# Down-projection bias of a MoE layer moved from the expert stage to the last stage, with two output buffers by chunk

## What is computed

```python
gu = xb @ w_gu[e] + b_gu[e]
gate = jnp.minimum(gu[:, :D_EXPERT], SWIGLU_LIMIT)
up = jnp.clip(gu[:, D_EXPERT:], -SWIGLU_LIMIT, SWIGLU_LIMIT)
act = (up + 1.0) * (gate * jax.nn.sigmoid(SWIGLU_ALPHA * gate))
y = act @ w_down[e] + b_down[e]
out[token] += gates[token, e] * y
```

## Time and profile before

| what | value |
|---|---|
| median of three executions | 2579.87 us |
| the profiled execution | 2585.97 us |
| its span from first to last instruction | 2584.3 us |
| busy PE, DVE, ACT, POOL | 2225.3, 1617.1, 1283.1, 578.6 us |
| stage 5 (868 to 942 us) | 74 us |
| stage 6 (942 to about 2500 us) | 1558 us |
| stage 7 (2513 to 2584.3 us) | 71.3 us |

### The profile page before, as it was taken

How to read it: one execution, slowest core, us unless ns; L and a number is a source line. 1 busy time by engine, 2 the same in 40 slices (tenths; PEclk the granted TensorE clock), 3 DMA queues, 4 the chain that set the end, 5 groups by cost and what they waited for, 6 DMA issues and landing times. The chain is left out here.

```text
span 2584.3 us, 38014 instructions
## 1 busy us (share of the span) xinstructions
PE 2225.3 (86%) x11995; PEld 1936.6 (75%) x11996; DVE 1617.1 (63%) x1973; ACT 1283.1 (50%) x1692; POOL 578.6 (22%) x610
## 2 busy tenths in 40 slices
PE   4899949598979429999999999999999999999960
PEld 3788837488868328897799889898777898788950
DVE  4320037474542526787866786786788867887746
ACT  4121124253432025666765675666676666766640
POOL 1430014331210241122211131121232311322114
PEclk9999979585789659999999999999999999999985
DMA  4122130322333166799987798796999978999768
GB/s 141 45 107 100 59 94 21 71 62 66 115 125 115 63 178 221 252 304 302 358 288 232 252 346 271 252 303 228 323 357 362 361 244 269 356 318 300 258 201 363
DMA packets 453456, 560.97 MB, mean 217 GB/s; under 512 B 62804, under 2 KB 342357, under 8 KB 453397
## 3 DMA queue, kind: packets, MB, share of 16 engines
q1 hardware_dynamic: 440373, 517.46, 61.2%
q0 software_dynamic: 13024, 42.75, 4.7%
HBM read 504.73 MB, written 55.35 MB: 217 GB/s over the span
## 5 line engine op out<-in xcount | busy, mean ns | idle before, releaser
L1511 DVE TENSOR_TENSOR VL<-RAW,VH 128x2048 fp32r<-128x2048 f32 x389 | 887.7, 2287 | 152.5 <-ACT VH L1506 149.7
L1506 ACT ACTIVATE VH<-RAW 128x2048 fp32r<-128x2048 f32 x390 | 725.9, 1907 | 110.3 <-DMA RAW<-in_expert_w_gate_up 70.3
L1909 PE MATMUL banks<-T,VH 128*128 128x384 f32 x1920 | 551.0, 361 | 19.0 <-DVE yb L1812 7.9
L1911 PE MATMUL banks<-T,VL 128*128 128x192 f32 x1680 | 422.5, 251 | 0.0
L1909 PEld LDWEIGHTS banks<-T,VH 128*128 128x128 f32 x1920 | 355.2, 189 | 25.1 <-issue 25.1
L1911 PEld LDWEIGHTS banks<-T,VL 128*128 128x128 f32 x1680 | 323.0, 192 | 0.0
L167 PE MATMUL banks<-VH,T 128*128 128x512 f32 x544 | 212.4, 391 | 0.0
L166 PE MATMUL banks<-VL,T 128*128 128x512 f32 x544 | 212.4, 390 | 0.0
L165 PE MATMUL banks<-VH,T 128*128 128x512 f32 x544 | 212.0, 390 | 0.0
L165 PE MATMUL banks<-VH,A 128*128 128x512 f32 x512 | 202.1, 395 | 5.2 <-DVE A L1749 5.1
L167 PE MATMUL banks<-VH,A 128*128 128x512 f32 x512 | 200.5, 392 | 0.0
(11 more groups left out here) (319 smaller groups left out, 4197.4 us busy)
## 6 DMA issues: line engine op xcount, KB each, us to landing
RAW<-in_expert_w_gate_up SPq DMA_DIRECT2D x264, 1024.0 KB
RAW<-in_expert_w_down SPq DMA_DIRECT2D x130, 1024.0 KB
dY<-yb SPq DMA_DIRECT2D x98, 128.0 KB
RAW<-in_w_in SPq DMA_DIRECT2D x6, 2048.0 KB, 8.6
dY<-zeros SPq DMA_DIRECT2D x17, 512.0 KB, 6.0
dY<-yb SPq DMA_DIRECT2D x32, 256.0 KB
xin<-in_x SPq DMA_DIRECT2D x8, 512.0 KB
qks<-dK SPq DMA_DIRECT2D x16, 256.0 KB
```

Source lines behind the costliest of these rows:

```text
L1506: act.activation(VH[:, i, ks], RAW[:, i, ks], ACT.Copy).then_inc(s_hi, 1)
L1511: dve.tensor_tensor(VL[:, i, ks], RAW[:, i, ks], VH[:, i, ks].bitcast(f32), ALU.subtract).then_inc(s_w, 1)
L1909: last = pe.matmul(o[:, 0:2 * NW], VH[:, c % 3, k, col], T2[:, k], start=k == 0, stop=k == KT - 1)
L1911: pe.matmul(o[:, HI_ALL], VL[:, c % 3, k, col], T2[:, k, HI_ALL], start=False, stop=False)
```

## The change

The bias table of stages 5 and 6 holds only the gate/up bias. In stage 5 DVE also builds `G`, each token's gates laid out over the 32 experts. In stage 6 the down product's first matmul opens its accumulation, there is no bias matmul in chunks 4 and 5, `s_bu` is raised by the bias matmul of chunk 3 (narrow) or near the end of the gate/up products (wide), and both output buffers are chosen by chunk (`yb` for 128 rows, a new `yl` for the left-over rows). Stage 7 loads the down bias three times, splits it and the gates, turns the gates on PE, multiplies, and adds the product to `acc` before the expert rows. `G` and `hot_e` lie on constants that later stages don't read. The diff, cut to its core:

```diff
 def stage5():
-                    for j in range(3):
-                        sp.dma_start(bias_rows(braw[32 * g:32 * g + NE], j, j + 3 * (g // 2)), bias_of(j + 3 * (g // 2))).then_inc(s_braw, 16)
+                    for j in range(2):
+                        sp.dma_start(bias_rows(braw[32 * g:32 * g + NE], j), bias_of(j + 2 * (g // 2))).then_inc(s_braw, 16)
...
-                dve.tensor_tensor(g4[:], g4[:], bc(gsum[:].unsqueeze(2), [P, TT, TOPK]), ALU.mult)
+                link(dve.tensor_tensor(g4[:], g4[:], bc(gsum[:].unsqueeze(2), [P, TT, TOPK]), ALU.mult))
+                link(dve.tensor_tensor(prod[:], sel[:], bc(g4[:].rearrange("p t k -> p (t k)").unsqueeze(2), [P, TT * TOPK, NE]), ALU.mult))
+                dve.tensor_reduce(G[:], prod[:].rearrange("p (t k) e -> p t e k", k=TOPK), X, ALU.add)
...
 def stage6():
-                                sp.dma_start(dY[...], yb[0:height(h), h]).then_inc(s_st[h], 16)
+                                sp.dma_start(dY[...], (yb[:, c % 2], yl[0:UN, c % 2])[h]).then_inc(s_st[c % 2], 16)
...
-                        act.wait_ge(s_st[0], s * 32 + (32 if c > GU else 16))
-                        act.activation(yb[:, 0], ps[2 * (c % 2)], ACT.Copy).then_inc(s_ea, 1)
+                        act.wait_ge(s_st[c % 2], s * 32 + 16)
+                        act.activation(yb[:, c % 2], ps[2 * (c % 2)], ACT.Copy).then_inc(s_ea, 1)
...
-                        dve.wait_ge(s_st[1], s * 32 + (32 if c > GU else 16))
-                        dve.tensor_tensor(yb[0:UN, 1], ps[2 * (c % 2) + 1][0:UN], yfold, ALU.add).then_inc(s_yl, 1)
+                        dve.wait_ge(s_st[c % 2], s * 32 + 16)
+                        dve.tensor_tensor(yl[0:UN, c % 2], ps[2 * (c % 2) + 1][0:UN], yfold, ALU.add).then_inc(s_yl, 1)
...
                 def narrow(s):
-                        biased = bias_in(o, c, P)
                         if c < GU:
+                            biased = bias_in(o, c)
+                            if c == GU - 1:
+                                biased.then_inc(s_bu, 1)
                             product(s, o, c, T2, range(KT)).then_inc(s_mm, 2)
...
-                            biased.then_inc(s_bu, 1)
                             product(s, o, c, A2, range(KT)).then_inc(s_mm, 2)
...
                 def wide(s):
+                        if i == G2 - 1:
+                            used.then_inc(s_bu, 1)
                         last.then_inc(s_mm, 1)
...
-                        bias_in(o, c, P)
...
-                        left_product(o, c, range(KT - 1))
-                        biased = pe.matmul(o[0:UN], hot_e[:, c // 3, 0:UN], btab[:, (c % 3) * CH:(c % 3 + 1) * CH], start=False, stop=False)
-                        if c == NCH - 1:
-                            biased.then_inc(s_bu, 1)
-                        left_product(o, c, [KT - 1]).then_inc(s_mm, 1)
+                        left_product(o, c, range(KT)).then_inc(s_mm, 1)
...
 def stage7():
+                for g in range(3):
+                    sp.dma_start(bdr[NE * g:NE * g + NE], b_dn).then_inc(s_bd, 16)
...
+            @block.scalar
+            def _(act):
+                act.wait_ge(s_bd, 48)
+                act.activation(bd3[0:3 * NE], bdr[0:3 * NE], ACT.Copy).then_inc(s_bhi, 1)
+                act.wait_ge(s_gT, 1)
+                act.activation(GT[0:3 * NE], pair(3, S)[0:3 * NE], ACT.Copy).then_inc(s_gt, 1)
+            @block.tensor
+            def _(pe):
+                pe.wait_ge(s_g3, 3)
+                for t in range(TT):
+                    last = pe.transpose(pair(3, S)[0:3 * NE, tok(t)], G3[:, t].bitcast(f32), ident[:])
+                last.then_inc(s_gT, 1)
+                pe.wait_ge(s_gt, 1)
+                pe.wait_ge(s_blo, 1)
+                for t in range(TT):
+                    if t >= 3:
+                        pe.wait_ge(s_xb, t - 2)
+                    for j in range(2):
+                        last = pe.matmul(ps[2 * (t % 3) + j], GT[0:3 * NE, tok(t)], bd3[0:3 * NE, j * CH:(j + 1) * CH], start=True, stop=True)
+                    last.then_inc(s_yb, 1)
...
             def _(dve):
+                dve.tensor_copy(G3[:, :, 0:NE], G[:]).then_inc(s_g3, 1)
+                dve.wait_ge(s_g3, 1)
+                dve.tensor_copy(G3[:, :, 2 * NE:3 * NE], G3[:, :, 0:NE].bitcast(f32)).then_inc(s_g3, 1)
+                dve.tensor_tensor(G3[:, :, NE:2 * NE], G[:], G3[:, :, 0:NE].bitcast(f32), ALU.subtract).then_inc(s_g3, 1)
+                dve.wait_ge(s_bhi, 1)
+                low = slice(2 * NE, 3 * NE)
+                dve.tensor_tensor(bd3[low], bdr[low], bd3[low].bitcast(f32), ALU.subtract).then_inc(s_blo, 1)
                 for t in range(TT):
                     dve.wait_ge(s_x[t % 2], 16 * (t // 2 + 1))
+                    dve.wait_ge(s_yb, t + 1)
+                    dve.tensor_tensor(acc[:, t], acc[:, t], pair(t % 3, D), ALU.add).then_inc(s_xb, 1)
+                    dve.wait_ge(s_xb, t + 1)
                     dve.wait_ge(s_k[t % YR], 16 * TOPK * (t // YR + 1))
```

More of the change, by code:

```diff
@@ L1276, in layer_kernel @@
     tokr = r5.take("tokr", [P, P])
-    braw = r5.take("braw", [P, 3 * CH])
+    braw = r5.take("braw", [P, 2 * CH])
+    G = Region(A_CONST + 2 * P * 4, KB).take("G", [P, TT, NE])
     diag = r5.take("diag", [P, SSB + 1])
@@ L1413, in _ @@
                 dve.wait_ge(s_bT, 1)
-                for q, n in ((0, 6), (1, 2)):
-                    dve.tensor_copy(btT[:, :, 6 * q:6 * q + n], ps[4 + q][:, 0:2 * n * NE].rearrange("p (g i e) -> p g i e", g=2, i=n))
+                for q in range(2):
+                    dve.tensor_copy(btT[:, :, 4 * q:4 * q + 4], ps[4 + q][:, 0:8 * NE].rearrange("p (g i e) -> p g i e", g=2, i=4))
                 dve.wait_ge(s_e, 1)
@@ L1441, in _ @@
                         c, j = i // 2, i % 2
-                        rows, at = slice(64 * (c // 3), 64 * (c // 3) + NE), (c % 3) * CH + g * HC + j * P
-                        q, n = c // 3, 6 - 4 * (c // 3)
-                        last = pe.transpose(ps[4 + q][:, (g * n + i % 6) * NE:(g * n + i % 6 + 1) * NE], braw[rows, at:at + P], ident[rows, rows])
+                        rows, at = slice(64 * (c // 2), 64 * (c // 2) + NE), (c % 2) * CH + g * HC + j * P
+                        last = pe.transpose(ps[4 + c // 2][:, (4 * g + i % 4) * NE:(4 * g + i % 4 + 1) * NE], braw[rows, at:at + P], ident[rows, rows])
                 last.then_inc(s_bT, 1)
@@ L1463, in layer_kernel @@
     yb = r6e.take("yb", [P, 2, CH])
-    btab = r6e.take("btab", [P, 3 * CH], f32r)
-    hot_e = r6e.take("hot_e", [P, 2, P], f32r)
+    yl = r6e.take("yl", [P, 2, CH])
+    btab = r6e.take("btab", [P, 2 * CH], f32r)
+    hot_e = Region(A_CONST, KB).take("hot_e", [P, 2, P], f32r)
     r6t = Region(A_TR, 4 * KB)
@@ L1493, in bias_of, with bias_rows @@
     def bias_of(c):
[L1495 to L1502, removed]
+        return b_gu.rearrange("e (g n) -> e g n", g=2)[:, :, c * HC:(c + 1) * HC]
+    def bias_rows(rows, j):
+        return rows[:, j * CH:(j + 1) * CH].rearrange("p (g n) -> p g n", g=2)
     def split_hi(act, i, hf):
@@ L1839, in product @@
                             pe.wait_ge(s_w, s * N2 + (2 * c + 1 + k // HK))
-                        last = mm3(pe, o, left[:, k, HI[0]], left[:, k, LO[0]], VH[:, c % 3, k], VL[:, c % 3, k], False, k == KT - 1)
+                        last = mm3(pe, o, left[:, k, HI[0]], left[:, k, LO[0]], VH[:, c % 3, k], VL[:, c % 3, k], c >= GU and k == 0, k == KT - 1)
                     return last
@@ L1848, in left_product, with bias_in @@
                     return last
-                def bias_in(o, c, m):
-                    return pe.matmul(o, hot_e[:, c // 3, 0:m], btab[:, (c % 3) * CH:(c % 3 + 1) * CH], start=True, stop=False)
+                def bias_in(o, c):
+                    return pe.matmul(o, hot_e[:, c // 2], btab[:, (c % 2) * CH:(c % 2 + 1) * CH], start=True, stop=False)
                 def turned(s, c):
@@ L1907, in wide @@
                                 if k == KT - 1:
[L1908 removed]
+                                    used = pe.matmul(o[:, HI_ALL], VL[:, c % 3, k, col], T2[:, k, HI_ALL], start=False, stop=False)
                                 last = pe.matmul(o[:, 0:2 * NW], VH[:, c % 3, k, col], T2[:, k], start=k == 0, stop=k == KT - 1)
@@ L1943, in layer_kernel @@
     acc = r7.take("acc", [P, TT, D])
+    G3 = r7.take("G3", [P, TT, 3 * NE], f32r)
+    GT = r7.take("GT", [P, S], f32r)
+    bdr = r7.take("bdr", [P, D])
+    bd3 = r7.take("bd3", [P, D], f32r)
     def stage7():
```

17 lines of the change are left out of this document (8 added, 9 removed).

## The result

The changed kernel took 2541.61 us in the median of four executions (2537.75 to 2544.77), the kernel before 2579.61 us beside it (2572.61 to 2588.82): a ratio of 0.985, 95% interval 0.9815 to 0.9885. It is faster by 38.0 us, the forecast was 30.5. The profiled execution took 2539.39 us.

What follows compares the result with a forecast made beforehand. PE was taken to bound the expert stage, with runs of narrow blocks at their weight stream's limit. Terms -13.9 - 16.8 - 2 + 2.2 = -30.5 us, from the median 2579.87, gave 2549.4 us, range 2538 to 2564.

Steps and rivals of the forecast that it cites:

- Wide bias matmuls: Expert stage: each wide block loses four bias matmuls, 60 in all at 0.23 us, 13.9 us less, from above 17.
- The pause after wide blocks: Expert stage: PE's waits for hot_e at 13 boundaries behind wide blocks go, 16.8 us less, ends 14 and 19.2.
- the floor of 0.2 us: Boundaries behind wide blocks: PE's own share of the pause, taken to stay at each after hot_e is released early.
- Narrow bias matmuls: Narrow blocks: of 34 removed, only chunk 4's in about 9 of 17 blocks count, 2 us less, ends 0 and 7.8.
- Two output buffers: Wide blocks' last chunk: ACT's 74.6 us of waits for the store leave the path, priced at nothing.
- Routing: Routing stage: DVE's added work, about 3 us, is covered because POOL's scatter sets the end: nothing, +-1 us.
- Last stage: Last stage: 0.95 us of loads plus 1.3 us of uncovered sums over five tiles, +2.2 us, ends +0.9 and +5.
- B: Rival, behind wide blocks: another release or PE's branch path keeps the pause; only matmuls go, -13.7, 2566 us; chance 0.13.
- C: Rival, narrow blocks: the removed narrow matmuls count in full, -36.3, 2544 us; chance 0.12.
- D: Rival, last stage: all eight sums uncovered, 11.4 us in place of 2.2, 2558.6 us; chance 0.08.
- F: Rival, expert stage: freed PE time turns into waits for rounding or activations, last stage's 2.2 us added, 2582 us; chance 0.06.
- E: Rival, narrow blocks: hot_e holds up DVE through the port shared with POOL, +54 us, 2633 us; chance 0.04.

Runs made afterwards that it cites:

- The release alone: Kernel before, all 162 bias matmuls kept, down bias given its own one-hot so hot_e is freed early: expert stage 1516.1 us against 1538.0, median 2555.26.
- The late release: Changed kernel with the release of hot_e put back to chunk 5, no bias matmul back: expert stage 1527.1 us, median 2567.09, ratio 0.9967.

## Why the prediction was right, point by point

The forecast was 2549.4 us in a range of 2538 to 2564, and the median 2541.61 lies in it. The direction, the places and the order of the terms were right. One size was not, that of the pause behind wide blocks, and the last stage's term had the right size for the wrong reason. That the pause was taken too small is most of the 7.5 us by which the forecast missed the gain.

- **Wide bias matmuls, -13.9.** Measured 13.9, by putting sixty back. The step from start to start was the price, not the 0.39 us that a row shows as duration. The Trainium skill, TensorE: Matmul & The Clock Gate, section Back-to-back issue gap, gives a sustained 131 ns for 512 columns, which would be 7.9 us; the runs show 0.23 us each, so the trace does not agree. By the same section of the Trainium skill the formula for an isolated matmul, N/2.4 + 2.5 ns, gives an estimate of 216 ns, and that is near. The upper end of 0.33 us was read from the earlier trace rows as a step behind transposes, but that step is behind a pause. Behind transposes the step is 0.31 to 0.34 us in both kernels, after a bias matmul and, in the changed kernel, after the first product: so the product inherits it, as the prediction said.
- **The pause after wide blocks, -16.8.** This is the term that was mis-sized. The release alone measured -21.9. The last matmul ahead of the wide-to-wide boundary of the earlier trace rows, in the kernel before, is

```profile
1349.12 0.40 PE L1847 MATMUL banks<-VH,A 128*128 128x512 f32 x1
```

By steps that pause was 1351.10 - 1349.12 - 0.23 = 1.75 us, where I took the bracket's 1.58; and the floor of 0.2 us is not there, since the step over a boundary is 0.23 like any other. 6 x 1.75 + 7 x (1.39 + 0.17) = 21.4. Both errors have one root: the bracket counts from the modelled end of the last matmul, 0.17 us after the next could have started. The first wide-to-wide boundary gave nothing, as said ("issue", 3.4 us before, 4.6 after).
- **Whose wait it was.** `hot_e` for all thirteen, against the label "DVE yb". The late release brings each of them back, the early one alone removes them.
- **Narrow bias matmuls, -2.** Measured -1.3 by the stage, which is near the noise, and -1.6 by the blocks: 0.23 in each of seven, not of "about 9". Rows of narrow blocks stayed at 38.5 us and 360 GB/s, as forecast.
- **Two output buffers, nothing.** True of the buffers by themselves (two are 1.5 us longer than one in the kernel before, 2.4 longer with the late release) and false with the early release, where one buffer costs 8.7 us. The prediction said that they keep the saved PE time from turning into that wait, and went on to price POOL's earlier gather at "same bytes: nothing". That step failed: with the same bytes but ahead of the store, the gather makes the wait for the store longer. In the kernel as changed this is covered, so the sum did not suffer.
- **Routing, 0.** Measured -0.2.
- **Last stage, +2.2.** Measured +2.0, but of other parts: 0.95 for loads and 1.3 for sums were forecast, and 1.5 is there without the sums, while no cost of the sums shows. That the total came out is luck. The step "0.25 us of each is uncovered" fell: without sums DVE only waits for rows.

The sum of terms is -21.9 - 13.9 - 1.3 = -37.1 for the expert stage, whose traces differ by 37.8 (36.5 with the changed kernel's second trace).

**The rivals.** B (the pause stays) fell by the boundaries, C by the 1.3 us, D by the +2.0, F by all of it. C's number, 2544, is nearer to the 2541.61 than the forecast's, but by chance: its 7.8 us for the narrow matmuls were not there, and the 5.1 us by which the pause had been taken too small happened to fill most of their place. E, the port, needed 1.8 us more in each narrow block, and they did not get longer. In a narrow block of the changed kernel POOL builds `hot_e` at 1256.61,

```profile
1256.61 2.94 POOL L1622 TENSOR_SCALAR hot_e<-rowkey,ecur 128x256 fp32r<-128x256 f32 x1 [0.20 <-POOL ecur L1620]
```

and DVE's split beside it takes what it takes everywhere:

```profile
1256.46 2.28 DVE L1510 TENSOR_TENSOR VL<-RAW,VH 128x2048 fp32r<-128x2048 f32 x1
```

In all 17 narrow blocks `hot_e` takes 2.94 to 2.99 us, and all 384 splits of the stage take 2.28 to 2.30. By the Trainium skill, SBUF — State Buffer, section Who interferes with whom, a DVE instruction with two SBUF inputs contends with a POOL instruction that reads SBUF, and the order of issue decides who blocks. The trace agrees as far as it shows the case: the split began first, and POOL was the one held (2.94 us where it takes 1.05 in a wide block). A case in which POOL was first was not seen.

## What to carry to other kernels

A buffer that is rebuilt for the next round and freed by the last instruction of this one is a pause in every round; giving its last reader another source can be worth more than the work saved. Price removed matmuls by the step from start to start, and a pause by the step over it less a normal step, since the idle figure and its label can be short and name a neighbour. When something is released earlier, ask what its engine issues next and which transfer that now stands in front of: a second buffer that is worth nothing today may be what the early release needs.

## What the runs showed that was not expected

- Stage 3 took 240.3 to 270.1 us in traces of kernels that are alike there, the shorter the higher the granted clock, 0.76 to 0.65. Of the 19.2 us by which the spans of the changed kernel's two traces differ it makes 18.9. The longest, from the run with the two buffers alone, whose profiled execution was 2603.08 us:

```profile
479.10:749.20 270.10, 231.10 (x1248) 215.51 (x1248) 142.70 (x234) 115.06 (x265) 61.62 (x67) 0.65 0.27 74
```

- A gather issued 0.36 us ahead of a store lengthened ACT's waits for that store to 120.1 us in 15, against 91.4 with the gather held back, and the blocks behind wide ones by 8.4 us against 0.8.
- The idle time in the brackets fell 0.17 us short of the measured loss at each wide boundary.
